# Other PSUM banks for three half groups of a two-block expert item, one transpose step later

## The reference

```python
def expert_block(args):                       # up to 128 rows of one expert at a time
    tok, e = args
    xb = u[tok]                               # gathered rows of the normed activations
    gu = xb @ w_gu[e] + b_gu[e]               # 1024 -> 2048: gate half and up half
    gate = jnp.minimum(gu[:, :D_FF], SWIGLU_LIMIT)
    up = jnp.clip(gu[:, D_FF:], -SWIGLU_LIMIT, SWIGLU_LIMIT)
    act = (up + 1) * gate * jax.nn.sigmoid(SWIGLU_ALPHA * gate)
    return act @ w_down[e] + b_down[e]        # 1024 -> 1024
out = out.reshape(p_rows, -1) * buf_g[:, None]
return jnp.zeros_like(u).at[buf_tok].add(out)
```

## Time and profile before

| what | value |
|---|---|
| median of 3 runs | 2210.99 us (2210.34 to 2217.0) |
| the profiled execution's own time | 2210.34 us |
| its span on the core | 2208.3 us |
| granted TensorE clock over the span | 0.978 of full |
| PE busy | 2133.2 us, 97% of the span |
| PEld (weight loads) busy | 1811.5 us, 82% |
| DVE busy | 1706.5 us, 77% |
| ACT busy | 1373.6 us, 62% |
| POOL busy | 408.2 us, 18% |
| DMA queue q1 | 61.2% of the 16 engines' time, 504.89 MB |

### The profile page before, as it was taken

How to read it: one execution, slowest core, us unless ns; L and a number is a source line. 1 busy time by engine, 2 the same in 40 slices (tenths; PEclk the granted TensorE clock), 3 DMA queues, 4 the chain that set the end, 5 groups by cost and what they waited for, 6 DMA issues and landing times. The chain is left out here.

```text
span 2208.3 us, 35903 instructions
## 1 busy us (share of the span) xinstructions
PE 2133.2 (97%) x11230; PEld 1811.5 (82%) x11231; DVE 1706.5 (77%) x2127; ACT 1373.6 (62%) x1752; POOL 408.2 (18%) x436
## 2 busy tenths in 40 slices
PE   7999999988959999999999999999999999999998
PEld 7987777767848998898898898988889998889884
DVE  5426667776658777979979978779997778998897
ACT  4324655544447566757857757567775667776675
POOL 0000000002342121213213213212321222221120
PEclk9999999999969999999999999999999999999996
DMA  4111101207859776979979979669997769998897
GB/s 162 44 48 34 58 34 44 101 31 229 181 185 343 248 241 248 377 265 349 382 263 353 377 259 352 236 243 380 373 382 267 252 229 332 388 364 336 290 370 283
DMA packets 106797, 548.41 MB, mean 248 GB/s; under 512 B 18071, under 2 KB 28824, under 8 KB 51834
## 3 DMA queue, kind: packets, MB, share of 16 engines
q1 hardware_dynamic: 88138, 504.89, 61.2%
q0 software_dynamic: 18608, 42.85, 8.1%
HBM read 516.45 MB, written 41.47 MB: 253 GB/s over the span
## 5 line engine op out<-in xcount | busy, mean ns | idle before, releaser
L2431 DVE TENSOR_TENSOR wl<-raw,wh 128x2048 fp32r<-128x2048 f32 x423 | 959.1, 2287 | 44.0 <-PE sums L2188 26.8
L2292 ACT ACTIVATE wh<-raw 128x2048 fp32r<-128x2048 f32 x425 | 804.7, 1912 | 113.2 <-PE sums L2188 39.4
L2172 PE MATMUL sums<-wh,xx 128*128 128x512 f32 x832 | 325.8, 392 | 0.9 <-issue 0.9
L2171 PE MATMUL sums<-wl,xx 128*128 128x512 f32 x832 | 325.6, 391 | 0.0
L2170 PE MATMUL sums<-wh,xx 128*128 128x512 f32 x832 | 325.3, 391 | 0.0
L2103 POOL DMA_INDIRECT h_dram<-y,pairs_mine x47 | 120.8, 2570 | 769.1 <-DVE y L2525 449.2
L2170 PE MATMUL sums<-wh,al 128*128 128x512 f32 x560 | 226.7, 405 | 0.6 <-DVE al L2516 0.3
L2172 PE MATMUL sums<-wh,ah 128*128 128x512 f32 x560 | 219.1, 391 | 0.0
L2171 PE MATMUL sums<-wl,ah 128*128 128x512 f32 x560 | 218.5, 390 | 0.0
L2171 PEld LDWEIGHTS sums<-wl,xx 128*128 128x128 f32 x832 | 156.9, 189 | 34.0
L2172 PEld LDWEIGHTS sums<-wh,xx 128*128 128x128 f32 x832 | 156.7, 188 | 33.4
(11 more groups left out here) (402 smaller groups left out, 4174.6 us busy)
## 6 DMA issues: line engine op xcount, KB each, us to landing
raw<-in_w_experts SPq DMA_DIRECT2D x426, 1024.0 KB, 6.5
raw<-in_w_chan SPq DMA_DIRECT2D x20, 512.0 KB, 3.3
o_gate<-in_x SPq DMA_DIRECT2D x8, 512.0 KB, 5.9
raw<-in_w_out SPq DMA_DIRECT2D x8, 512.0 KB, 5.5
ht<-in_x SPq DMA_DIRECT2D x8, 512.0 KB, 5.9
h_dram<-ht SPq DMA_DIRECT2D x8, 512.0 KB, 9.0
u_dram<-ut SPq DMA_DIRECT2D x8, 512.0 KB, 10.1
h_all<-h_dram SPq DMA_DIRECT2D x8, 512.0 KB, 6.8
```

What stands on the lines that cost most here:

```text
L2171: pe.matmul(out, hi[:, n, :], w_lo[:, kk, :], start=False, stop=False)
L2172: last = pe.matmul(out, hi[:, n, :], w_hi[:, kk, :], start=False, stop=half == 1 and kk == 3)
L2292: nc.scalar.activation(wh[ch % HIGHS][:, :, :], raw[ch % RAW][:, :, :], ACT.Copy).then_inc(h_split.sem, 1)
L2431: dve.tensor_tensor(wl[ch % LOWS][:, :, :], raw[ch % RAW][:, :, :], wh[ch % HIGHS][:, :, :], ALU.subtract).then_inc(l_split.sem, 1)
```

## The change

Three edits, all for two-block items.

1. The table `pairs`: (2, 1), the up part of group 2, moves from `x_ps` to `sums` banks 2 and 3, which (1, 0) has used before; (3, 0) moves from those banks to `a_ps`; (3, 1) moves from `a_ps` to `x_ps`. The waits in `tiles_free`, `biases` and before `turn_next` are set to match.
2. `turn_act(i, 0, ...)`, the four transposes of the activated group 0, stands after chunk 3 instead of after chunk 2.
3. `pick_columns` is gone; `pick`, which runs for all 35 items and once ahead of the loop, writes `own_bias` right behind `sel`.

```diff
-        pairs = {(1, 0): k.sums[:, 2:4, :], (1, 1): a_ps[:, :, :],
-                 (2, 0): k.sums[:, 0:2, :], (2, 1): x_ps[:, :, :].rearrange("p (a n) b -> p a (n b)", a=2),
-                 (3, 0): k.sums[:, 2:4, :], (3, 1): a_ps[:, :, :]}
+        pairs = {(1, 0): k.sums[:, 2:4, :], (1, 1): a_ps[:, :, :], (2, 0): k.sums[:, 0:2, :], (2, 1): k.sums[:, 2:4, :],
+                 (3, 0): a_ps[:, :, :], (3, 1): x_ps[:, :, :].rearrange("p (a n) b -> p a (n b)", a=2)}
...
             def biases(i, g, blocks):
                 if g < 2:
                     pe.wait_ge(y_read.sem, y_read.at(i, g - 1))
-                elif blocks == 2:
-                    pe.wait_ge(gate_ready.sem, gate_ready.at(i, g - 1))
                 else:
                     pe.wait_ge(gu_read.sem, gu_read.at(i, g - 1))
...
                 elif (g, part) == (2, 0):
                     pe.wait_ge(gu_read.sem, gu_read.at(i, 1))
                 elif (g, part) == (2, 1):
+                    pe.wait_ge(gate_ready.sem, gate_ready.at(i, 2))
+                elif (g, part) == (3, 0):
+                    pe.wait_ge(gu_read.sem, gu_read.at(i, 2))
+                elif (g, part) == (3, 1):
                     pe.wait_ge(a_low.sem, a_low.at(i, 1))
-                elif (g, part) == (3, 0):
-                    pe.wait_ge(gate_ready.sem, gate_ready.at(i, 2))
-                elif (g, part) == (3, 1):
-                    pe.wait_ge(gu_read.sem, gu_read.at(i, 2))
...
-                    by_weights(i, 2)
+                    for ch in range(2, 4):
+                        by_weights(i, ch)
                     turn_act(i, 0, blocks)
-                    for ch in range(3, 8):
+                    for ch in range(4, 8):
                         by_weights(i, ch)
...
                 if blocks == 2:
-                    pe.wait_ge(gu_read.sem, gu_read.at(i, 3))
+                    pe.wait_ge(gu_read.sem, gu_read.at(i, 4))
                 turn_next(i)
...
                 nc.scalar.activation(sel[:, :, :].rearrange("p a b -> p (a b)")[:, 0:P + H],
-                                     k.c["pick"][:, ds(e, 1)].broadcast_to([P, P + H]), ACT.Copy).then_inc(sel_ready.sem, 1)
-
-            def pick_columns(i):
-
-                e = act.value_load(k.items[0:1, ds(i, 1)], min_val=0, max_val=N_EXPERTS - 1)
-                nc.scalar.activation(own_bias[:, :], k.b_columns[:, :, ds(e, 1)].rearrange("p a b -> p (a b)"), ACT.Copy)
+                                     k.c["pick"][:, ds(e, 1)].broadcast_to([P, P + H]), ACT.Copy)
+                nc.scalar.activation(own_bias[:, :], k.b_columns[:, :, ds(e, 1)].rearrange("p a b -> p (a b)"),
+                                     ACT.Copy).then_inc(sel_ready.sem, 1)
...
                     high_second(i)
-                    pick_columns(i)
```

## The result

The changed kernel takes 2250.83 us (median of 4 runs, 2246.41 to 2255.02) against 2211.87 (4 runs): ratio 1.0172, 95% interval 1.0144 to 1.0200. It is slower, as forecast, but by more: 11 over the forecast of 2239.5 and above the range's 2247. The profiled execution took 2250.22, with a span of 2248.2. Two of the signs of being wrong that the prediction names are there: matmuls behind most of the pauses cost nearly double, and the granted clock of the loop is 0.98, not 0.99.

What follows compares the result with a forecast made beforehand. TensorE's own instructions were taken to bound the kernel, busy 1519.61 of 1530.00 in the loop. Pause and restart 2.51 less pace 0.08 gave 2.43, times 12 = 29.2, on 2210.34: 2239.5, range 2232 to 2247.

Steps and rivals of the forecast that it cites:

- signs of being wrong: TensorE's new loop wait missing, more than once an item or at `turn_next`, or matmuls behind the pause costing double.
- The pause: At part (2, 1), TensorE waits for the clamp of group 1's gate part: 2.41 in each two-block item.
- The chain: From the transposes through ScalarE's reading, VectorE's `low_act(0)`, `low(6)`, folds and clamp: TensorE starts at 5.14, asks at 2.73.
- pause and restart together: At part (2, 1): pause 2.41 plus restart 0.10, together 2.51 per two-block item.
- rival B: A second hold later in the item, VectorE fallen back against `turn_next`'s cover: 2251.5, chance 0.06.
- The clock: Granted clock of the expert loop stays at 0.99 after the pauses; no loss priced in the likeliest case.
- rival A: The pause drops TensorE's clock to the low level, 3.3 lost after each of 12 pauses: 2279, chance 0.05.
- The pace: Matmul pairs of two-block items: chunk 3 takes 4.56, gain 0.08 per item, bounds 0 and about 0.5.
- `own_bias`: priced at nothing: Written in `pick`, at most 0.23 more on ScalarE in each of 35 items, hidden; 5.3 if unhidden.
- The other terms: (3, 0) in `a_ps` hidden, (3, 1) in `x_ps` done in time, `turn_next` with 3.01 of cover: priced at nothing.
- The direction: Whole kernel: slower 0.93, same 0.04, faster 0.03.

Runs made afterwards that it cites:

- the shorter: Changed kernel with VectorE's `low(6)` moved behind the clamp of group 1's gate part in two-block items: 2242.66 against 2209.29, ratio 1.0155.
- the longer pause: Changed kernel with two VectorE instructions of no use ahead of the folds of group 1's gate part: 2277.67 against 2209.29, ratio 1.0308.
- the repeat: The changed kernel measured once more, against the kernel before: 2250.19 against 2209.29, ratio 1.0180.
- The filled pause: Changed kernel with 12 matmuls of no use on TensorE ahead of the wait for part (2, 1): 2235.58 against 2207.84, ratio 1.0127.
- the version without a pause: Changed kernel with `low(6)` behind the clamp and `high(8)` behind the copies of group 1's gate part: 2211.87 against 2209.29, ratio 1.0012.
- `own_bias` in its old place: Changed kernel with `low(6)` and `high(8)` moved behind group 1's gate clamp and copies, and `pick_columns(i)` back: 2207.66 against 2208.85, ratio 0.9996.

## Why the prediction was wrong

*The pause: right.* Its place, its cause and its length held. The chain gave 5.14 from the transposes and measured 5.14 in the items. The idle time was forecast at 2.41 and is recorded as 2.27, since TensorE is shown busy until the modelled end of the last of the eight pairs, 0.14 later than the start of the next would be (708.61 + 0.25 = 708.86). The price of pause and restart together, forecast at 2.51, can be taken from two runs that differ only in the banks and `own_bias`: 30.23 in an item without a fall, 27.72 with the transposes moved alone, so 2.51. It came twelve times, there was no second hold at `turn_next` (rival B), and the shorter, the missing and the longer pause moved the time the way the chain says.

*The clock: the step that failed.* The prediction took the clock to stay at the high level after each pause, priced its loss at nothing and gave rival A 0.05. In the changed kernel it fell at 9 of the 12 pauses, which cost 15.7, and at 9 of 12 again in the repeat. The one piece of evidence against rival A was read too short. It was the pause of 2.55 at 516.45, with the first three matmuls behind it, all quick. Read on in the same trace, and the clock falls 1.5 behind the restart (timeline of TensorE, and the granted clock of the stretch):

```profile
517.74 0.39 PE L133 MATMUL o_ps<-wo_h,mh 128*128 128x512 f32 x1
517.96 0.58 PE L131 MATMUL o_ps<-wo_h,ml 128*128 128x512 f32 x1
518.34 0.63 PE L132 MATMUL o_ps<-wo_l,mh 128*128 128x512 f32 x1
...
521.32 0.44 PE L133 MATMUL o_ps<-wo_h,mh 128*128 128x512 f32 x1
521.60 0.40 PE L131 MATMUL o_ps<-wo_h,ml 128*128 128x512 f32 x1
```

```profile
518.00:521.40 3.40, 3.40 (x10) 2.63 (x9) 1.60 (x2) 1.19 (x3) 3.33 (x2) 0.50 0.97 389
```

So the pause that was to speak against rival A spoke for it, as far as a single pause can, and it held the price too: nine matmuls take 3.64 from 517.96 to 521.60, where at some 0.23 each they would take 2.1, which is 1.5 lost; a fall at a pause of 2.27 costs 1.59. Rival A's own size was wrong: it took 3.3 from the start of the loop, where the clock had been low since 617 (0.50 from 617 to 657.9), long before the loop. Falls as they were measured, in number and in price, give 15.7 rather than 0 or 40. The Trainium skill's section on HAM oscillation ("TensorE: Matmul & The Clock Gate") tells of a loop whose waits put the clock back in every turn. The runs agree for pauses of 3.46 (12 of 12); with pauses of 1.78 and 2.27 it was 7 and 9 of 12.

*The pace: right in its sign, too small.* Chunk 3 took 4.56 (701.43 to 705.99), the number taken. But all pairs behind the transposes ran at 0.285 too, which the prediction kept as a bound only: 0.42 per item rather than 0.08. Per item without a fall the sum gave 2.43 and the trace has 2.51 - 0.42 = 2.09, so 25.1 instead of 29.2. The filled pause, which leaves that and `own_bias`, measured 27.7 over the kernel before, with 25.7 in groups 1 to 3. On 2210.34 the 25.1 and the 15.7 are 2251.1, against 2250.2 for the execution; that it comes so close is in part luck, since the differences outside groups 1 to 3 nearly cancel.

*`own_bias`: priced at nothing*, measured at 0 to 3. *The other terms* (the banks, (3, 0), (3, 1), `turn_next`): nothing, as forecast.

*Range and chances.* The direction was given 0.93 and came. The range was too narrow, since it held the clock at one level for all 12 items; a mixed case, some falls out of 12 at some price, was missing between the forecast and rival A.

What stays open: why the clock falls at some pauses of 2.27 and not at others of the same length; and why the pairs run at 0.290 behind transposes that follow chunk 2 and mostly at 0.285 behind transposes that follow chunk 3. With the transposes behind chunk 2, pairs alternate 0.287 and 0.293 through all five chunks, with the old banks and the new; the same alternation comes back behind the short wait in one item of the version without a pause and in five with `own_bias` in its old place. So it looks like a rhythm that the engine falls into; no run took it apart.

## What to carry to other kernels

A buffer that is freed earlier in the program is not freed earlier in time when its readers are queued in order behind something the same edit makes late: follow the releasing chain on each engine from the moved instruction on, and compare it with the moment of the next use. On a TensorE that is always busy price a recurring pause as its length and restart plus the chance of a low clock at it. Take that chance from more than one pause, and read each one well past the first matmuls behind it. If the pause can't be avoided, try work of no use in it: here 12 matmuls that fitted in it added nothing and took the falls away. And when a combined edit loses, run its parts alone: one of these three is a small gain.

## What the runs showed of the hardware that was not expected

- Pauses of 0.1, 1.8, 2.27 and 3.46 on a TensorE that is otherwise always busy came with the low clock in 0, 7, 9 (twice) and 12 of 12 items. With 1.7 of the 2.27 filled with matmuls: 0 of 12. The two ends of this row are clear; that 1.8 and 2.27 differ is not shown.
- The clock need not fall in the pause. In one item TensorE restarts at 966.49 at full speed and the pairs turn slow 0.65 later, and in the trace before it was 1.5 behind the restart at 516.45:

```profile
966.49 0.44 PE L2213 MATMUL sums<-xx,wh 128*128 128x384 f32 x1 [2.27 <-DVE tg L2473]
...
967.05 0.25 PE L2214 MATMUL sums<-xx,wl 128*128 128x192 f32 x1
967.14 0.47 PE L2213 MATMUL sums<-xx,wh 128*128 128x384 f32 x1
967.41 0.36 PE L2214 MATMUL sums<-xx,wl 128*128 128x192 f32 x1
967.57 0.58 PE L2213 MATMUL sums<-xx,wh 128*128 128x384 f32 x1
```

- Which items have a fall differed between the two profiled executions of the changed kernel. Its executions spread over 8.6 (2246.41 to 2255.02), but those of the kernel before, which has no such falls in its loop, spread over 6.7 beside them.
